# One layer of a hybrid decoder trunk: raw tokens turned, their scale applied with the modulation

## The reference

```python
mod = silu(c) @ w_ada + b_ada                      # c is one row of 1024
shift, mscale, gate = split(mod, 3)
h = rms_norm(x, norm_gain) * (1.0 + mscale) + shift
proj = h @ w_in                                    # 1024 x 1024 by 1024 x 4376
q, kv, nsa_gl, z_attn, u, z_ssm, merge_gl = split(proj, IN_OFFSETS)
# u goes into the state space model, z_ssm gates its result,
# q and kv go into the attention; the output is rms_norm(x + gate * (merged @ w_out))
```

## Time and profile before

| | us |
|---|---|
| median of 3 runs | 931.57 |
| lowest, highest | 931.38, 932.0 |
| profiled execution, its own time | 932.66 |
| its span | 930.9 |
| PE busy | 889.9 |
| PE weight load busy | 731.8 |
| DVE busy | 526.0 |
| ACT busy | 417.4 |
| POOL busy | 207.0 |

### The profile page before, as it was taken

The page is one execution under the profiler, slowest core; times in us unless marked ns, Lnnn a source line. Parts: engine busy times, 40 slices in busy tenths (PEclk is TensorE's granted clock), DMA queues, the critical chain, the costliest instruction groups (busy, mean ns, idle before and its releaser), DMA issues. The chain is left out here.

```text
span 930.9 us, 14393 instructions
## 1 busy us (share of the span) xinstructions
PE 889.9 (96%) x5553; PEld 731.8 (79%) x5553; DVE 526.0 (57%) x1098; ACT 417.4 (45%) x830; POOL 207.0 (22%) x203
## 2 busy tenths in 40 slices
PE   2899999999999999999999999999999999999996
PEld 2578999789899777777777776888888888887885
DVE  2652374459775798798798796731222122237454
ACT  5743232522345578778778878721111111133221
POOL 3359912111000102212212212255550000000000
PEclk9999999999999999999999999999999999999999
DMA  9956052041010000000000001333232121123222
GB/s 304 327 141 114 1 119 71 1 94 47 1 47 1 1 1 1 2 1 1 2 1 1 2 1 35 86 97 108 63 108 63 34 62 29 66 115 136 91 91 90
DMA packets 61091, 59.44 MB, mean 64 GB/s; under 512 B 10240, under 2 KB 53824, under 8 KB 61008
## 3 DMA queue, kind: packets, MB, share of 16 engines
q1 hardware_dynamic: 58768, 53.90, 19.9%
q0 software_dynamic: 2000, 4.54, 1.8%
q10 hardware_dynamic: 256, 0.09, 0.0%
HBM read 52.69 MB, written 5.24 MB: 62 GB/s over the span
## 5 line engine op out<-in xcount | busy, mean ns | idle before, releaser
L1248 DVE TENSOR_TENSOR plo<-pt,phi 128x512 fp32r<-128x512 f32 x192 | 106.2, 568 | 37.1 <-ACT phi L851 36.7
L851 ACT ACTIVATE pt<-bank 128x512 f32<-128x512 f32 (+1 forms) x208 | 99.5, 478 | 51.5 <-PE bank L1777 50.9
L1777 PE MATMUL bank<-q,k 128*128 128x512 f32 (+3 forms) x384 | 102.4, 348 | 0.4 <-ACT phi L851 0.4
L851 ACT ACTIVATE phi<-bank 128x512 fp32r<-128x512 f32 (+1 forms) x208 | 99.6, 479 | 0.0
L1777 PEld LDWEIGHTS bank<-q,k 128*128 128x128 f32 x384 | 62.9, 189 | 13.6 <-ACT phi L851 4.2
L650 POOL TENSOR_TENSOR qa<-qa,otmp 128x256 f32<-128x256 f32 x32 | 27.2, 851 | 198.6 <-DVE otmp L1248 198.6
L1567 DVE TENSOR_REDUCE mx<-slc_max 128x1 f32<-128x128 f32 (+3 forms) x64 | 48.2, 753 | 11.1 <-PE slc_max L1777 9.3
L1777 PE MATMUL bank<-ht_hi,dhi 128*128 128x512 f32 x128 | 49.8, 389 | 0.0
L1777 PE MATMUL bank<-ht_lo,dhi 128*128 128x512 f32 x128 | 49.8, 389 | 0.0
L1777 PE MATMUL bank<-ht_hi,dlo 128*128 128x512 f32 x128 | 49.8, 389 | 0.0
L1248 DVE TENSOR_TENSOR dtm<-bank,dsig 128x512 f32<-128x512 f32 x16 | 11.1, 692 | 64.3 <-ACT dsig L851 64.3
(11 more groups left out here) (447 smaller groups left out, 2591.5 us busy)
## 6 DMA issues: line engine op xcount, KB each, us to landing
ada<-in_w_ada SPq DMA_DIRECT2D x16, 512.0 KB, 9.7
draw<-in_w_in SPq DMA_DIRECT2D x16, 512.0 KB, 3.7
wraw<-in_w_in SPq DMA_DIRECT2D x7, 1024.0 KB, 5.3
xs<-in_x SPq DMA_DIRECT2D x8, 512.0 KB, 9.3
gstage<-in_w_ada POOLq DMA_DIRECT2D x16, 256.0 KB, 3.0
oraw<-in_w_out SPq DMA_DIRECT2D x8, 512.0 KB, 6.4
xr<-in_x SPq DMA_DIRECT2D x8, 512.0 KB, 4.1
out<-yr SPq DMA_DIRECT2D x7, 512.0 KB, 2.9
```

The lines of the kernel that those rows point to most:

```text
L851: return nc.scalar.activation(o, i, fn, **kw)
L1248: return V.tensor_tensor(o, a, b, op)
L1777: return T.matmul(o, l, r, start=start, stop=stop, **kw)
```

## The change

- Raw tokens are turned tile by tile as they land: two groups of four transposes for a tile, into four PSUM banks in turn. DVE copies all 16 groups to `xt`. Nothing scales `xs` any more.
- The token scale is formed once, after the eighth square. DVE spreads it over a diagonal, `rdiag`; PE multiplies this by a matrix of ones, which puts each token's scale into every partition; ACT copies the result to `rsb`.
- `h_scaled` multiplies by `g1` and by `rsb`. The shift moves: `h_high` adds it as the bias of an Identity activation, `h_lo` adds it as it subtracts.
- `state_input` waits for `ht_hi` first and for `wlo` and `ht_lo` only ahead of the products which need them; the order of the six is both column tiles for each pair.
- Sums and columns of the later blocks are put elsewhere among the first products: sums of j = 1 behind block 0, columns of j = 1 inside block 1, sums of j = 2 and 3 inside blocks 2 and 4, their columns behind these blocks. The turning of `cld` goes behind block 5, the copies to `ct` ahead of the last `ht_hi`.
- `keep_running` issues products whose result nobody reads: three ahead of the wait for `rdiag`, one ahead of the sums of j = 1.

```diff
@@ -479,7 +481,7 @@
                KS_: False, KW_: False}
 
     NH = KT + 1
-    SUM_BANK = (2, 1, 4, 5)
+    SUM_BANK = (2, 4, 5, 4)
     COLUMN_BANK = (0, 6, 7, 6)
...
                 a(junk[:, :], xs[:, i, :], ACT.Square, accum_out=ss[:, i:i + 1]).then_inc(s_sq, 1)
-                if i % 4 == 3:
-                    act.wait_ge(s_var, i // 4 + 1)
-                    a(rs[:, i - 3:i + 1], ss[:, i - 3:i + 1], ACT.Sqrt).then_inc(s_sd, 1)
-            for cc in range(NC_HALF):
-                for k in range(0, KT, 2):
-                    n = KT * cc + k
-                    act.wait_ge(s_xtr, n + 1)
-                    a(xt[:, k, cc * HALF:(cc + 1) * HALF], bank[4 + n % 4]).then_inc(once("xta"), 1)
-                if cc == 0:
-                    act.wait_ge(once("pcol"), 1)
-                    a(dt_[:, :], pcol[:, 32:40], ACT.Exp).then_inc(once("dt"), 1)
-                    a(scol[:, :, :], pcol[:, 48:56].unsqueeze(2).to_broadcast([P, KT, 32]), ACT.Silu).then_inc(s_silu, 1)
+            act.wait_ge(s_var, 1)
+            a(rs[:, :], ss[:, :], ACT.Sqrt).then_inc(s_sd, 1)
+            act.wait_ge(once("pcol"), 1)
+            a(scol[:, :, :], pcol[:, 48:56].unsqueeze(2).to_broadcast([P, KT, 32]), ACT.Silu).then_inc(s_silu, 1)
+            for hf in range(2):
+                act.wait_ge(s_xtr, 2 * ST + hf + 1)
+                a(rsb[:, hf * HALF:(hf + 1) * HALF], bank[6 + hf]).then_inc(once("xta"), 1)
+            a(dt_[:, :], pcol[:, 32:40], ACT.Exp).then_inc(once("dt"), 1)
...
                 for m, cols in enumerate(h_parts(k)):
                     act.wait_ge(s_h32, m + 1 if k == 0 else k + 2)
-                    a(ht_hi[:, k, cols], xt[:, k, cols]).then_inc(s_hhi, 1)
+                    a(ht_hi[:, k, cols], xt[:, k, cols], ACT.Identity, bias=modc[:, k:k + 1]).then_inc(s_hhi, 1)
...
             a(whi[0][:, :, 0:256], wraw[:, :, 0:256]).then_inc(s_whi, 1)
             h_high(0)
-            for r in range(2):
-                act.wait_ge(once("ctr"), 1)
-                a(ct[r][:, :, :], bank[3][:, P * r:P * r + P].rearrange("p (t c) -> p t c", t=SSM_T)).then_inc(once("ctev"), 1)
+            h_high(1)
             modulation_rows(1)
-            h_high(1)
             act.wait_ge(once("pw_arg"), 1)
             a(pw[:, 1, :, :], pw[:, 1, :, :], ACT.Exp).then_inc(once("pw_fn"), 1)
             h_high(2)
             h_high(3)
+            modulation_rows(2)
             a(pw[:, 2, :, :], pw[:, 0, :, :], ACT.Sin, scale=SIN_2PI / 2).then_inc(once("pw_fn"), 1)
             a(pw[:, 3, :, :], pw[:, 0, :, :], ACT.Sin, scale=SIN_2PI).then_inc(once("pw_fn"), 1)
-            modulation_rows(2)
             h_high(4)
             h_high(5)
             modulation_rows(3)
             h_high(6)
+            for r in range(2):
+                act.wait_ge(once("ctr"), 1)
+                a(ct[r][:, :, :], bank[7][:, P * r:P * r + P].rearrange("p (t c) -> p t c", t=SSM_T)).then_inc(once("ctev"), 1)
             h_high(7)
...
+            def turned_tokens(i):
+
+                for hf in range(2):
+                    n = 2 * i + hf
+                    dve.wait_ge(s_xtr, n + 1)
+                    V.tensor_copy(xt[:, 4 * hf:4 * hf + 4, P * i:P * i + P], bank[4 + n % 4].rearrange("p (k t) -> p k t", k=4))\
+                        .then_inc(once("xtd"), 1)
+
+            for i in range(ST):
+                turned_tokens(i)
+                if i == 2:
+                    dve.wait_ge(s_prow, 16 * 6)
+                    V.tensor_copy(prow[32:40, :].rearrange("t (g s) -> t g s", g=2),
+                                  dtr[32:40, :].unsqueeze(2).to_broadcast([SSM_T, 2, SS])).then_inc(once("dtx"), 1)
+                elif i == 3:
+                    dve.wait_ge(once("ptr"), 1)
+                    V.tensor_copy(pcol[:, :], bank[3][:, 0:PROWS]).then_inc(once("pcol"), 1)
+            dve.wait_ge(s_sq, ST)
+            V.tensor_scalar(ss[:, :], ss[:, :], 1.0 / D_MODEL, EPS, ALU.mult, ALU.add).then_inc(s_var, 1)
+            dve.wait_ge(s_sd, 1)
+            V.reciprocal(rs[:, :], rs[:, :]).then_inc(s_rs, 1)
+            dve.wait_ge(s_rs, 1)
+            dve.wait_ge(s_id, 16)
+            tt(rdiag[:, :, :], ident[:, :].unsqueeze(1).to_broadcast([P, ST, P]),
+               rs[:, :].unsqueeze(2).to_broadcast([P, ST, P]), ALU.mult).then_inc(s_xn, 1)
             dve.wait_ge(once("pcol"), 1)
...
@@ -1304,15 +1296,17 @@
             def h_scaled(k):
 
                 for cols in h_parts(k):
-                    V.tensor_scalar(xt[:, k, cols], xt[:, k, cols], g1[:, k:k + 1], modc[:, k:k + 1], ALU.mult, ALU.add)\
-                        .then_inc(s_h32, 1)
-
-            dve.wait_ge(once("xta"), 8)
+                    V.scalar_tensor_tensor(out=xt[:, k, cols], in0=xt[:, k, cols], scalar=g1[:, k:k + 1], in1=rsb[:, cols],
+                                           op0=ALU.mult, op1=ALU.mult).then_inc(s_h32, 1)
+
+            dve.wait_ge(once("xta"), 2)
+            dve.wait_ge(once("xtd"), 2 * ST)
 
             def h_lo(k):
                 for m, cols in enumerate(h_parts(k)):
                     dve.wait_ge(s_hhi, m + 1 if k == 0 else k + 2)
-                    tt(ht_lo[:, k, cols], xt[:, k, cols], f(ht_hi[:, k, cols]), ALU.subtract).then_inc(s_hlo, 1)
+                    V.scalar_tensor_tensor(out=ht_lo[:, k, cols], in0=xt[:, k, cols], scalar=modc[:, k:k + 1],
+                                           in1=f(ht_hi[:, k, cols]), op0=ALU.add, op1=ALU.subtract).then_inc(s_hlo, 1)
...
                     pe.wait_ge(s_silu, 1)
-                if j == 2:
-                    pe.wait_ge(once("xta"), 8)
...
                 pe.wait_ge(once("mrow"), j + 1)
                 if j >= 1:
-                    pe.wait_ge(once("xtd"), 8)
+                    pe.wait_ge(once("xta"), 2)
                     pe.wait_ge(once("modc"), j)
...
+            for i in range(ST):
+                pe.wait_ge(s_x[i], 16)
+                for hf in range(2):
+                    n = 2 * i + hf
+                    if n >= 4:
+                        pe.wait_ge(once("xtd"), n - 3)
+                    for q in range(4):
+                        ins = tr(bank[4 + n % 4][:, P * q:P * q + P], xs[:, i, P * (4 * hf + q):P * (4 * hf + q) + P])
+                    ins.then_inc(s_xtr, 1)
+                if i == 3:
+                    pe.wait_ge(s_prow, 16 * 6)
+                    pe.wait_ge(once("dtx"), 1)
+                    tr(bank[3][:, 0:PROWS], prow[0:PROWS, :], PROWS).then_inc(once("ptr"), 1)
+            def keep_running(n, b):
+
+                for _ in range(n):
+                    mm(bank[b], onesq[:, :], xs[:, 0, 0:HALF], True, True)
+
+            pe.wait_ge(once("vc0"), 1)
+            keep_running(3, 1)
+            pe.wait_ge(s_xn, 1)
+            pe.wait_ge(once("xtd"), 2 * ST)
+            for hf in range(2):
+                mm(bank[6 + hf], onesq[:, :], rdiag[:, 4 * hf:4 * hf + 4, :].rearrange("p i t -> p (i t)"), True, True)\
+                    .then_inc(s_xtr, 1)
             def bank_free(n):
 
                 m = n - 4
...
             modulation_sums(0)
-            pe.wait_ge(once("pcol"), 1)
-            pe.wait_ge(once("cld"), 16 * 2 * SSM_T)
-            for r in range(2):
-                ins = tr(bank[3][:, P * r:P * r + P], cld[r][:, :])
-            ins.then_inc(once("ctr"), 1)
             modulation_columns(0)
-            modulation_sums(1)
+
+            def state_columns():
+
+                pe.wait_ge(once("cld"), 16 * 2 * SSM_T)
+                for r in range(2):
+                    ins = tr(bank[7][:, P * r:P * r + P], cld[r][:, :])
+                ins.then_inc(once("ctr"), 1)
+
             pe.wait_ge(s_whi, 1)
-            pe.wait_ge(once("wlo0"), 1)
 
             def state_input(k, cc):
 
-                if k == 4:
-                    pe.wait_ge(s_wlo, 1)
-                if k == 0:
-                    pe.wait_ge(s_hlo, cc + 1)
-                else:
-                    pe.wait_ge(s_hlo, k + 2)
-                if k == 0 and cc == 1:
-                    pe.wait_ge(once("mrow"), 2)
-                    pe.wait_ge(once("ctev"), 2)
-                for ct_ in range(2):
-                    i = 2 * ct_ + cc
-                    cs, ts = slice(P * ct_, P * ct_ + P), slice(cc * HALF, (cc + 1) * HALF)
-                    parts = ((whi[0], ht_hi), (whi[0], ht_lo), (wlo[0], ht_hi))
-                    for m, (l, r) in enumerate(parts):
-                        ins = mm(unit_bank(i), l[:, k, cs], r[:, k, ts], k == 0 and m == 0, k == KT - 1 and m == 2)
+                part_no = cc + 1 if k == 0 else k + 2
+                ts = slice(cc * HALF, (cc + 1) * HALF)
+                pe.wait_ge(s_hhi, part_no)
+                for m, (l, r) in enumerate(((whi[0], ht_hi), (wlo[0], ht_hi), (whi[0], ht_lo))):
+                    if m == 1 and k in (0, 4):
+                        pe.wait_ge(once("wlo0") if k == 0 else s_wlo, 1)
+                    elif m == 2:
+                        pe.wait_ge(s_hlo, part_no)
```

(62 more changed lines are left out.)

2 lines of the change are left out of this document (removed).

## The result

| | before | after |
|---|---|---|
| median, us (12 runs each, side by side) | 931.68 | 933.76 |
| lowest, highest | 931.31, 932.07 | 932.99, 934.7 |
| ratio after to before | | 1.0022, interval 1.0014 to 1.003 |
| profiled execution, own time | 932.66 | 933.15 |
| its span | 930.9 | 931.3 |

I forecast 930.0 in 928.7 to 932.4. The median lies 3.8 us above the forecast and outside the range. The runs of after fall in two groups of six, 932.99 to 933.46 and 934.06 to 934.7.

A forecast was written before the change was run, and what follows sets the result against it. PE's dense stream was taken to bound the kernel: first product 8.4 us earlier, mostly spent waiting for block 1's landing, state input ending at 64.7 instead of 66.30, net 1.6 us, so 931.57 becomes 930.0; range 928.7 to 932.4.

The forecast's parts named there:

- rival D: Opening: the clock does not rise while PE only transposes; 3.4 us lost there, 933.4 us; chance 0.08.
- The first product: Opening: the projection's first product starts at 29.7 us, 8.4 earlier, behind the first weights' split starting at 27.1.
- `ht_hi` through Identity needed no table load: ACT's high part with a bias: taken at the copy's 1.04 us; upper bound a 1.28 table load before some.
- PE waited 1.76 behind the columns of block 1 (forecast 1.8): Ahead of block 2's first product: PE waits 1.8 us for modulation, scaling and high part, covered by one half block.
- `cp` was no new wait: Past the second weight chunk: POOL's last `cp` step stays at 102.9 us, with 1.2 us to spare before PE reads it.
- rival B: Opening: the clock falls in PE's 3.6 us without work; 0.9 to 2.4 us lost, 930.9 to 932.4; chance 0.20.
- 0.23 for each of block 0's twelve products: Behind the first product: twelve products 0.23 us apart, with short waits for low parts, ending at 32.9.
- the middle part: From block 1's sums at 33.9 to the state input's end, claimed at 64.7 instead of 66.30, net 1.6 us.
- A: The forecast itself: 929.2 to 930.7, varying by modulation chains 0.2 quicker or dearer and block 1's landing; chance 0.55.
- My waits there, 1.35: New waits behind columns of blocks 2 and 3: 0.45 and 0.4, then 0.1 and 0.4; 1.35 us together.
- this 1.09: Profiled execution before stood 1.09 us above the 931.57 median; the forecast 931.1 execution was thus taken as median 930.0.

The follow-up runs named there:

- e1_fill: The changed kernel with three more filler products directly behind the turning of block 0's columns; 932.77 us, ratio 1.001.
- e2_nofill: The changed kernel with all four of the change's own filler products taken out; 932.98 us, ratio 1.0018.
- e4_fill_both: The changed kernel with three fillers behind block 0's columns and two in the wait ahead of channel block 2; 932.17 us, ratio 1.0004.
- e3_sums_first: The changed kernel with three fillers behind block 0's columns, and sums of blocks 2 and 3 moved ahead of channel blocks 2 and 4; 929.35 us, ratio 0.9973.
- e0_again: The changed kernel itself, unaltered, run again for a second trace; 933.8 us, ratio 1.0022 to the kernel before.
- e10_five_fillers: The changed kernel with five fillers behind block 0's columns, sums of blocks 2 and 3 ahead of channel blocks 2 and 4; 929.63 us, ratio 0.9981.
- e7_sums_only: The changed kernel with sums of blocks 2 and 3 moved ahead of channel blocks 2 and 4, no fillers added; 930.31 us, ratio 0.9984.
- e5_fill_second: The changed kernel with two fillers ahead of channel block 2 only, the opening's idle stretch left; 933.69 us, ratio 1.002.

## Why the prediction was wrong, step by step

**What came as forecast.** The transposes take the fast pace after nothing but transposes: 9.36 to 11.00 is 0.2 apart, after 11.00 it is 0.13. That is against rival D and against the rule of the Trainium skill (TensorE: Matmul & The Clock Gate, "Part 4: PE-mode transpose") that the full rate does not engage for transposes; this trace disagrees with it as before's did. It is the pace that shows it: the granted clock reads 1.00 at the slow pace too (6 to 10 us). The first product stood right behind `whi`, 29.00 against 29.7, because the chunk landed 0.8 earlier. `ht_hi` through Identity needed no table load (ACT's loads, at 22.99 and 47.20, stand ahead of other work), in agreement with the Trainium skill (ScalarE: Activation LUTs, "Table sets: the hidden batching unit"). PE waited 1.76 behind the columns of block 1 (forecast 1.8), and `cp` was no new wait, ready at 104.8 and read at 106.35. It did not stay, though: I had it ready at 102.9, and it came 1.8 later.

**The step that failed first: the clock over the opening's idle stretch.** I took 0.23 for each of block 0's twelve products, and argued against rival B that "the 1.78 us of idleness before 38.06 did not lower it". That was a reason about another, shorter stretch. The only row of a stretch of this length was the one at the end, where the clock did fall after 3 us, and it spoke for B. The clock fell in both traces of after. Twelve products at 0.427 took 5.25 us instead of 2.8, the filler 1.23 instead of 0.86, and block 1's sums began at 35.48 instead of 33.9: 1.6 us. B's price of 0.9 to 2.4 was right; its chance was not. Its time, 930.9 to 932.4, was missed all the same, because it stands on the middle part and the base of A. By over 0.2% slower I gave only D, 0.08, and D did not happen: the side on which the time fell had no reason in my text that came true.

**The step nobody had: the same wait of 1.8 us.** I used the 1.78 us before 38.06 as proof that such a wait is harmless, and forecast a wait of 1.8 behind the columns of block 1 without asking it of the clock. That wait lowered it in the second trace of after and in `e1_fill`, by 1.3 to 1.4 us, and not in after's first trace or in `e2_nofill`, with 1.76 each. The rows around it do not separate the cases. In `e1_fill`, where the clock fell, PE is busy for 0.99 of 38 to 40 and 1.24 of 40 to 42. In after's first trace, where it held, it is 0.85 of 40 to 42 and 1.27 of 42 to 44, the same work 1.85 us later. In the kernel before, around the wait that did not matter:

```profile
34.00:36.00 2.00, 1.56 (x16) 0.26 (x8) 1.91 (x5) 1.01 (x2) 0.00 (x0) 1.00 1.11 349
36.00:38.00 2.00, 0.70 (x3) 0.65 (x4) 2.00 (x4) 0.96 (x4) 0.00 (x0) 1.00 1.10 349
38.00:40.00 2.00, 2.00 (x12) 1.65 (x12) 0.88 (x2) 1.47 (x2) 0.00 (x0) 1.00 1.10 349
```

Here a full stretch follows. But `e2_nofill` had 0.24 in 40 to 42 and kept the clock, and the same trace of before kept it through another wait of 1.71 us, with PE busy for 0.29 of 31 to 33. What decides in one execution and not in the next stays open.

**The terms of the sum behind block 1.** From its sums to the sums of block 2 I had 8.9 (33.9 to 42.8); measured 9.11 in after, 9.10 in `e4_fill_both` and `e2_nofill`. The rounding to `ht_hi` with a bias took 1.15 to 1.2 where I had 1.04. From block 2's sums to the end I had 21.9; measured 22.29, 22.26, 22.31. My waits there, 1.35, were 1.10 in the trace, the last one for `ht_hi` not counted. What I had left out is that a product behind a wait is followed only 0.34 later instead of 0.23 (51.70 to 52.04), four times, and 0.1 ahead of the sums, and the state columns, with that last wait, took 0.54 instead of 0.4. Together 0.6: the stretch took 31.4 where I had 30.8 and before had 31.9. So the gain of the middle part was 0.5, not the 1.1 of my sum.

**The base.** Before's trace was late at block 1 (34.36, the second one 33.63), and its own time stood 1.09 above the median. I carried this 1.09 over to the forecast. After's profiled execution stood 0.61 below its median. The 3.8 us between forecast and median are 2.05 in the profiled executions (933.15 against 931.1; at the end of the state input it is 2.2, 1.6 from the clock and 0.6 from the terms) and 1.7 in this carrying over. Whether the second fall makes part of that in some of the runs is not shown. Neither the clock's 1.6 nor these 1.7 alone would have put the median outside the range; the two together did, with the 0.6 of the terms on top.

**The decision that I never questioned.** I took the sums' new place as given and summed what it costs: 1.85 behind the first half, and a wait of 1.8 ahead of it. Side by side in my own text stood a wait of 1.8 us for columns and a work of 1.85 that depends on no column. `e3_sums_first` shows that moving the sums back is worth 2.8 us, more than everything else here, 1.7 of it from this pair. So rival R1 of `e0_again`, that the new waits and the moved sums make the loss, was the larger part of the truth, 2.8 us, and the clock the smaller, 1.6. A rival "the sums leave their cover" would have ended on the slower side: the kernel before runs them in that place.

**Not settled.** `e4_fill_both`, with no fall in its trace, is 0.5 above before although its stretch behind block 1 is 0.5 shorter. In the traces the difference is block 1's landing. Its last part, issued at nearly the same time (the line, then the time from issue to landing), in after and in `e4_fill_both`:

```profile
L538 SPq DMA_DIRECT2D ada<-in_w_ada x1: 2774/2774/2774, 21.8 to 21.8; - x1
DMA to landing us min/median/max: 11.1/11.1/11.1
```

```profile
L538 SPq DMA_DIRECT2D ada<-in_w_ada x1: 2747/2747/2747, 22.0 to 22.0; - x1
DMA to landing us min/median/max: 12.4/12.4/12.4
```

It landed at 32.9 and at 34.4. The six traces with the opening's fillers have 11.7 to 12.5 for this time, the five of the changed kernel without them 10.8 to 11.2, the three with the old opening 11.0 to 11.7, while the moved bytes hardly differ (334 GB/s and 335 near 30 us). So the fillers, or the higher clock that they keep, go with a later landing, which would give back about a microsecond of what they save. No run separates these from each other, nor from chance of the execution, and no cause is shown.

## What to carry to other kernels

Put filler work where PE idles longest, read from a trace of the changed kernel; ahead of fillers, look for real work that depends on nothing which that wait is for. An opening that ends in a landing is not won by starting earlier; follow the early start to the first wait on a DMA before counting a gain. Where the forecast is about 0.2%, take a second trace of the kernel before, since the first can be a microsecond off the median.

## What the runs showed of the hardware

- The granted clock fell behind a wait of 1.77 us with work around it (`e1_fill`, and the second trace of after), and did not behind 1.76 in two other executions. The place cost 1.3 to 1.4 us in the traces in which it fell. Whether it also makes the scatter of the runs is open: `e3_sums_first`, without such a wait, has 929.22 to 929.53, but `e10_five_fillers`, also without it, 929.33 to 930.59.
- The moment at which the transposes take the fast pace differs between executions of the same opening code: 3.2 us behind the first transpose in `e3_sums_first` (6.05 to 9.23), 5.1 in after (5.89 to 11.00), and over 5.2 in `e7_sums_only`, whose eight transposes at 13.76, behind a start at 8.59, still took 1.42 us. The granted clock reads 1.00 throughout, so this is read from the pace alone.
- `ident`, which the first transpose waits for, landed at 5.9 to 6.1 us in nine of the eleven traces with the new opening and at 8.6 in `e5_fill_second` and `e7_sums_only`. The row sums and fillers behind the last transposes began at 16.52 in after, at 18.57 in `e5_fill_second` and at 19.32 in `e7_sums_only`:

```profile
13.76 1.42 PE L1774 MATMUL bank<-ident,xs 128*128 128x128 f32 x8
...
19.32 2.74 PE L1771 MATMUL bank<-xs,onesq 128*128 128x512 f32 x6
```

- Block 1's last part landed between 32.8 (second trace of after) and 34.4 us (`e4_fill_both`), at the same place of the same queue. That is as much as the effect that was to be forecast.
